# Chunk steps and layer head of a two-layer attention and RWKV-7 trunk: four moves of work in the engines' queues

## What is computed

```
x <- LN(alpha*x + (sigmoid(gA)*attention(x) + sigmoid(gB)*rwkv7(x)) @ w_out)
x <- LN(alpha*x + conv_glu(x))

attention:  8 heads of 128 share one k and v; an indexer scores the keys,
            the 64 best scores of each row are kept, softmax over these
rwkv7:      16 heads of 64; for each token t
   state = state*w_t + (state @ -kk_t) b_t + v_t k_t ;  y_t = state @ r_t
   kk_t  = k*k_k / |k*k_k|  (norm over a head)
   w_t   = exp(-exp(-softplus(-(w0 + tanh(p_w) @ w2)) - 0.5))
```

## Time and profile before

| | before |
|---|---|
| median of 3 runs | 1269.19 us (1268.2 to 1271.25) |
| the profiled execution's own time | 1277.04 us |
| its span | 1274.8 us |
| PE busy | 1160.5 us (91%) |
| DVE busy | 785.9 us (62%) |
| ACT busy | 537.2 us (42%) |
| granted TensorE clock, mean | 0.964 of full speed |
| HBM traffic over the span | 128 GB/s |

### The profile page before, as it was taken

One profiled execution on the slowest core, in us unless ns is written; L12 is line 12 of the kernel. 1 busy time (PEld: TensorE's weight loads), 2 busy tenths in 40 slices (PEclk: granted clock), 3 DMA queues, 4 the chain that ended last, 5 costly groups with the idle time before them and its releaser, 6 DMA issues.

```text
span 1274.8 us, 29251 instructions
## 1 busy us (share of the span) xinstructions
PE 1160.5 (91%) x12328; PEld 1042.2 (82%) x12328; DVE 785.9 (62%) x1436; ACT 537.2 (42%) x938; POOL 50.6 (4%) x56
## 2 busy tenths in 40 slices
PE   7996989898988899999999969898989898999997
PEld 7775878787878799998797758787878887999985
DVE  1338557675747777775522565667667577777745
ACT  2232445453534455654212424344545434556531
POOL 0000000000000100000000000000000001000000
PEclk9988999999999899999999978999999998999999
DMA  7422222222336365556464212212222464555561
GB/s 268 147 74 79 68 76 69 76 68 75 102 116 207 118 220 182 183 188 205 144 201 149 81 44 68 77 66 76 68 68 102 144 209 149 194 182 182 187 208 68
DMA packets 45353, 165.38 MB, mean 130 GB/s; under 512 B 5136, under 2 KB 5392, under 8 KB 44976
## 3 DMA queue, kind: packets, MB, share of 16 engines
q1 hardware_dynamic: 42576, 154.02, 36.3%
q0 software_dynamic: 1504, 7.47, 1.8%
q10 hardware_dynamic: 1152, 2.10, 0.5%
HBM read 160.42 MB, written 3.15 MB: 128 GB/s over the span
## 4 chain that ended last, share of the span: by engine, by line
PE 76%; DVE 17%; ACT 3%; issue 3%; DMA 1%; POOL 0%; DVEq 0%; SPq 0%; ACTq 0%
PE ps L722 18%; PE ps L723 16%; PE ps L724 16%; PE ps L869 8%; PE ps L697 5%; PE ps L1028 3%; DVE ring_r L1516 3%; DVE keep L1934 1%; PE ps L1070 1%; PE ps L881 1%; DVE small L1932 1%; PE ps L798 1%; PE ps L770 1%; ACT mid_hi L1192 1%; DMA ring<-stream_dram 1%
## 5 line engine op out<-in xcount | busy, mean ns | idle before, releaser
L722 PE MATMUL ps<-x_tok_r,mid_hi 128*128 128x256 f32 x448 | 138.6, 309 | 15.0 <-DVE ring_r L1516 15.0
L723 PE MATMUL ps<-xT_r,mid_hi 128*128 128x256 f32 x448 | 127.6, 285 | 0.0
L724 PE MATMUL ps<-x_tok_r,ring_r 128*128 128x256 f32 x448 | 127.4, 284 | 0.0
L722 PEld LDWEIGHTS ps<-x_tok_r,mid_hi 128*128 128x128 f32 x448 | 86.2, 192 | 25.3 <-issue 12.6
L697 PE MATMUL ps<-xT,ring 128*128 128x256 f32 x448 | 102.8, 388 | 0.0
L697 PEld LDWEIGHTS ps<-xT,ring 128*128 128x128 f32 x448 | 86.3, 195 | 13.8 <-issue 1.6
L1516 DVE TENSOR_TENSOR ring_r<-ring,mid_hi 128x1024 fp32r<-128x1024 f32 x64 | 77.9, 1219 | 25.0 <-ACT mid_hi L1192 25.0
L723 PEld LDWEIGHTS ps<-xT_r,mid_hi 128*128 128x128 f32 x448 | 86.7, 193 | 0.0
L724 PEld LDWEIGHTS ps<-x_tok_r,ring_r 128*128 128x128 f32 x448 | 86.5, 193 | 0.0
L1633 DVE COPY_PREDICATED X_Y<-masks,ps 128x256 f32<-128x256 uint32 x80 | 35.3, 441 | 66.0 <-PE ps L869 54.7
L1192 ACT CAST mid_hi<-ring 128x1024 fp32r<-128x1024 f32 x64 | 67.2, 1054 | 12.7 <-PE ps L724 12.7
(11 more groups left out here) (443 smaller groups left out, 3394.8 us busy)
## 6 DMA issues: line engine op xcount, KB each, us to landing
ring<-stream_dram SPq DMA_DIRECT2D x281, 512.0 KB, 3.4
lora_w<-lora_dram POOLq DMA_DIRECT2D x2, 1536.0 KB, 7.2
W_bt<-rpar_dram POOLq DMA_DIRECT2D x4, 512.0 KB, 4.5
kt_V<-rpar_dram POOLq DMA_DIRECT2D x4, 512.0 KB, 5.4
x_tok<-x_dram SPq DMA_DIRECT2D x2, 512.0 KB, 4.6
v_saved_dram<-vs_dC ACTq DMA_DIRECT2D x4, 256.0 KB, 3.9
x_tok<-x_dram SPq DMA_DIRECT2D x1, 1024.0 KB, 5.3
vf<-v_saved_dram ACTq DMA_DIRECT2D x4, 256.0 KB, 3.6
```

The costliest lines, as they stand in the source:

```text
L722: pe.matmul(dst, lh, rh, start=start, stop=False)
L723: pe.matmul(dst, lh, rl, start=False, stop=False)
L724: return pe.matmul(dst, ll, rh, start=False, stop=stop)
```

## The change

Seven edits, all of them moves; no instruction is added or taken out.

1. Head of a layer, PE: `prep_1` comes first, then two dense pieces, then `prep_ss` and `prep_v`; `prep_rnx` comes one place on, ahead of pieces 6 and 7. On DVE `prep_decay` and `prep_pend` come ahead of `prep_ss`.
2. `prep_bk` comes ahead of `prep_v` on DVE, in the head and in the last chunk step.
3. Softmax: `att_norm` comes ahead of level 3 on DVE (it stood after it).
4. `prep_ss` of the next group moves on PE from gap 13 to gap 12 (`SQUARES`).
5. Chunk steps: the splits due in a step come ahead of the Q copy on ACT, and ahead of the S sums on DVE, right behind Zs and T; T itself comes right behind Zs.
6. `prep_rnx` of the next group moves on PE from behind Z(1) and its fill to behind y(0), ahead of Z(1).
7. ACT resets Y at a group's start before it waits for v.

The lists of semaphore steps follow the new order and are left out. On PE:

```diff
-LOGITS, Y_BACK, BONUS, PROBS, VALUES = 4, 7, 8, 11, 13
+LOGITS, Y_BACK, BONUS, PROBS, SQUARES, VALUES = 4, 7, 8, 11, 12, 13
...
                     fill(14 + 2 * c)
-                    if g + 1 < GROUPS and c == 1:
-                        prep_rnx(r + 1)
...
                     mm.then_inc(*pe_wkv.inc(r, f"y{c}"))
+                    if g + 1 < GROUPS and c == 0:
+                        prep_rnx(r + 1)
...
-                for k, p in enumerate((prep_ss, prep_1, prep_v, prep_rnT)):
-                    p(r0)
+                for k, ps_ in enumerate(([prep_1], [prep_ss, prep_v], [prep_rnT], [prep_rnx])):
+                    for p in ps_:
+                        p(r0)
                     for piece in first[2 * k:2 * k + 2]:
                         piece()
-                prep_rnx(r0)
...
-                        gaps[VALUES].append(lambda: prep_ss(r0 + g + 1))
+                        gaps[SQUARES].append(lambda: prep_ss(r0 + g + 1))
```

On ACT:

```diff
             def chunk(r, c):
+                mids_up_to(r // GROUPS, mids_by(GAPS * (r % GROUPS) + 13 + 2 * c))
                 act.wait_ge(*pe_wkv(r, f"Q{c}"))
                 act.copy(Qs[:, :, :], step64(3)).then_inc(*act_wkv.inc(r, f"Q{c}"))
...
+                    act.copy(Y, stack.unsqueeze(1).broadcast_to([P, NU, CH])).then_inc(*act_wkv.inc(r, "resetY"))
                     act.wait_ge(*(dve_prep(r, "v") if l else dve_dense(l, ("rkv", 3 * g + 2))))
-                    act.copy(Y, stack.unsqueeze(1).broadcast_to([P, NU, CH])).then_inc(*act_wkv.inc(r, "resetY"))
...
                         chunk(r, c)
-                        mids_up_to(l, mids_by(GAPS * g + 14 + 2 * c))
```

On DVE (`chunk_t` makes T; `chunk_s` no longer does):

```diff
-                prep_ss(r0)
                 prep_decay(r0)
                 prep_pend(r0)
+                prep_ss(r0)
                 topk(0)
                 prep_rn(r0)
                 topk(1)
                 prep_keys(r0)
                 prep_arc(r0)
+                prep_bk(r0)
                 prep_v(r0)
-                prep_bk(r0)
...
                     for lev in range(LEVELS):
+                        if lev == 3:
+                            att_norm(l, g)
                         if lev:
                             level(r, lev)
...
-                        if lev == 3:
-                            att_norm(l, g)
...
                         if c:
                             chunk_z(r, c)
+                            if c < NCH - 1:
+                                chunk_t(r, c)
+                            mids_up_to(l, mids_by(GAPS * g + 13 + 2 * c))
...
                             elif nxt:
+                                prep_bk(r + 1)
                                 prep_v(r + 1)
-                                prep_bk(r + 1)
+                        else:
+                            mids_up_to(l, mids_by(GAPS * g + 13))
                         if c < NCH - 1:
                             chunk_s(r, c)
...
-                        mids_up_to(l, mids_by(GAPS * g + 13 + 2 * c))
```

More of the change, by code:

```diff
@@ L504, in trunk @@
         pool_att = by_layer("pool_att", ["eps", "rs"])
-        pe_prep = Steps(sem("pe_prep"), [["ss", "zw", "za"] + (["zv"] if r >= GROUPS else []) + ["rnT", "rnx"]
+        pe_prep = Steps(sem("pe_prep"), [(["ss", "zw", "za"] if r % GROUPS else ["zw", "za", "ss"]) + (["zv"] if r >= GROUPS else []) + ["rnT", "rnx"]
                                          for r in range(R)])
@@ L509, in trunk @@
                                            + (["thv"] if r >= GROUPS else []) for r in range(R)])
-        dve_prep = Steps(sem("dve_prep"), [["ss", "s", "cum", "cp", "pend", "rnT", "kkn", "k2", "kb", "arc"]
-                                           + (["v1", "v2", "v"] if r >= GROUPS else [])
-                                           + ["bneg", "kp", "rkk"] for r in range(R)])
+        dve_prep = Steps(sem("dve_prep"), [(["ss"] if r % GROUPS else []) + ["s", "cum", "cp", "pend"]
+                                           + ([] if r % GROUPS else ["ss"]) + ["rnT", "kkn", "k2", "kb", "arc", "bneg", "kp"]
+                                           + (["v1", "v2", "v"] if r >= GROUPS else []) + ["rkk"] for r in range(R)])
         pool_prep = by_round("pool_prep", ["rn"])
@@ L1673, in chunk_z, with chunk_t @@
                 dve.tensor_tensor(Zs[:, :, :], step64(2), akV[:, c::NCH, :], ALU.add).then_inc(*dve_wkv.inc(r, f"Z{c}"))
+            def chunk_t(r, c):
+                dve.tensor_tensor(Sa[:, :, :], S[:, (c + 1) % 2, :, :], ktV[:, GB * c:GB * c + GB, :], ALU.add
+                                  ).then_inc(*dve_wkv.inc(r, f"T{c}"))
             def chunk_s(r, c):
@@ L1677, in chunk_s @@
                 if c:
-                    dve.tensor_tensor(Sa[:, :, :], S[:, (c + 1) % 2, :, :], own, ALU.add).then_inc(*dve_wkv.inc(r, f"T{c}"))
                     dve.wait_ge(*dve_wkv(r, f"T{c}"))
```

## The result

The changed kernel took 1234.3 us (median of 4 runs, 1231.38 to 1236.45), the kernel before 1270.22 (4 runs, 1268.2 to 1271.99) beside it: a ratio of **0.9716**, interval 0.969 to 0.9742, faster. In a later study the pair stood at 1233.04 and 1273.85, ratio 0.9676 (0.9651 to 0.9702). So the gain is 35.9 us by the one pair and 40.8 by the other; the forecast's sum was 39.2.

The account below looks back on a forecast made before the run. PE's work plus its idle places was taken to bound the kernel. Heads 10.4 and 8.4, softmax 5.4, chunk steps 8.8 and clock 6.2 sum to 39.2 us, so 1269.2 us becomes 1230 us, range 1218 to 1246.

Parts of the forecast that it names:

- Bounds: Whole kernel: time is PE's work plus its idle places; PE busy 91% of the span, with 76% of the chain.
- Head of layer 0: From PE's idle at 78.88 us to DVE's first merge: search 8.7 us earlier, grams' start-up 1.7 less, 10.4 us gained.
- Head of layer 1: Same reordering from 711.48 us: search 5.4 us earlier, `b_k` ahead of v 2.1 more, first merge 8.4 us earlier.
- 717.5: Sign for layer 1's head: in the profile after, the search for the best starts near 717.5 us.
- Softmax: Division ahead of level 3: 1.0 us gained in four groups, 0.7 in two, 5.4 us, between 0 and 9.3.
- Chunk steps: Split waits 11.5 us gained, less 1.8 for Z(1) behind `prep_rnx` and 0.9 for `y_sum`: 8.8 us, between 0 and 11.5.
- The clock: Low stretches behind softmax waits, group 2 of layer 0 (4.2 us) and two layer 1 groups (1.0 each), go: 6.2 us.
- the last low clock before 439 us lies in group 0: Sign in the profile after: among layer 0's groups, the last low clock before 439 us is in group 0.
- the clock does not come back: Rival: low stretches arise elsewhere as often as they vanish; 10.8 us of gain lost, 1241 us; chance 0.15.
- DVE did not become the bound: Rival that DVE, fuller in chunk steps 1 and 2, becomes the bound: 8.8 and 5.4 us go, 1244 us; chance 0.13.
- ACT's rounding never held up Q: Slower rival: rounding ahead of the Q copy waits for its slot, up to 2.27 us per step, 1285 us; chance 0.03.
- nothing waited for a slot's landing: Rival that the stream's slots land too late, removed waits return as DMA waits, time stays near 1269; chance 0.02.

Follow-up runs that it names:

- head_only: The kernel before with only the heads' new order, bneg and kp ahead of v there, and ACT's earlier Y reset: 1250.01 us, ratio 0.9812.
- u_chunk: The change with the chunk steps' splits put back behind the Q copy on ACT and behind S on DVE: 1245.71 us, ratio 0.9799.
- rn_first: The change with DVE's copy of rnT moved ahead of the S(0) sums: 1223.36 us, ratio 0.9625.
- u_rnx: The change with `prep_rnx` put back behind Z(1) and its fill: 1227.14 us, ratio 0.965.
- b_fill: The kernel before with idle PE products added in the wait for the softmax's division, groups 1 to 3: 1267.47 us, ratio 0.9965.
- fill_head: The change with idle PE products added in the heads' wait for `b_k`: 1233.18 us, ratio 0.9678.

## Why the prediction was right, and where it was not

1230 us was forecast, 1234.3 measured, inside the range and faster as expected. The sum was helped by errors that cancelled, as told below. By steps:

- *Bounds.* Right: the time went with PE's waits and its clock. Of the profiles' last stage (324.96 to 319.76) some 2.5 us lie at no place that the change touches: head_only, which has every wait of that stage's group as before, took 322.51. They belong to the executions.
- *Head of layer 0*, 10.4 us. The search was forecast for 84.9 and began at 84.21; the operand's wait came out at 2.0 instead of 1.4 us, and the first merge was 11.1 us earlier. *Head of layer 1*, 8.4: 5.8 us for the search (5.4 forecast), 9.0 for the merge. The sign "717.5" was put in the old kernel's time; what was gained ahead of it had to come off, and the search began at 693.62. Together 19.8 of 18.8.
- *Softmax*, 5.4: 5.5 by the waits. What was named as late next, X_Y, is what is there, 0.75 us in four groups and 0.38 in two.
- *Chunk steps*, 8.8. Taken apart it was less good. The splits: 11.5 forecast, and 16.4 - 6.7 in `ring_r` plus 2.7 - 1.2 in the waits without a releaser give 11.2; taken back, 11.4. The longer wait for `y_sum` in layer 1: 0.9 forecast; the entry grew by 0.3. The wait behind `prep_rnx`: "0.3 us are lost in each of six groups, 1.8 us" is right as a wait (0.26 each), but edit 6 as a whole measured 7.2 (3.3 by the other ratio), of which 1.6 are the wait and 1.5 a low stretch. This term was too small, since the low clock behind the new wait was not in it.
- *The clock*, 6.2. **This is the step that failed**: "With the waits at 0.8 us or less I let these go." The low time in heads and groups fell from 64.9 to 30.7 us, but low stretches of 3.4 us stand behind waits of 0.75 us for X_Y in groups 1 and 2 of layer 0, and behind the new 0.82 us wait at L811 in group 1 of layer 1. So group 1 of layer 0 gained 1.1 us where the forecast's terms for it come to 1.0 + 1.5 - 0.3 = 2.2, and group 2 gained 5.4 of 6.4. Three such stretches at about 1.5 us are 4.5 of the 6.2. Group 0, where I had let the low clock stand, went the other way: from the grams' operand on it had 20.5 us at 0.50 in each layer and has 10.2, and its stages gave 3.1 and 2.6 us where the forecast's terms for them come to 1.2 and 0.9. The sign "the last low clock before 439 us lies in group 0" was wrong: it lies in group 2.
- *The sum.* The errors are of both signs, so the sum stands, at 39.2 against 35.9 and 40.8. That is in part luck: what the clock did not give back in groups 1 and 2 it gave in group 0, for which the forecast had nothing. Taken back one at a time the parts give 19.2 + 7.8 + 11.4 - 7.2 = 31.2; what is missing to 35.9 is less than four intervals of about 3 us leave uncertain, and with the change at a ratio of 0.969 in that study the parts would make up the whole.

Of the rivals, "the clock does not come back" was half right: low stretches did arise at other places, behind shorter waits, and 1234.3 lies between the forecast and its 1241. DVE did not become the bound in the steps (S's waits are as short as they were, but for the 0.26 us at L811), ACT's rounding never held up Q, and nothing waited for a slot's landing. The section of the Trainium skill that the prediction cited (TensorE: Matmul & The Clock Gate, HAM oscillation — how this bites in real kernels) gives as its rule that only idle gaps longer than any wait in these groups bring the low clock. The runs speak against that: a 1.8 us wait had 0.58 behind it, filled it had 1.00, and two of the 0.75 us waits have 0.82 behind them. In u_chunk the same 0.75 us wait in group 1 of layer 0 has no low stretch behind it, so the wait's length alone does not decide. The same section of the Trainium skill takes half of a throttled time as the price, by which I estimate 1.7 us for 3.4. The trace is near: the change's two profiles have 60.92 and 62.38 for one stage without such a stretch and with one, and rn_first and u_rnx have 59.29 and 60.72, 59.49 and 61.05 for the like stages of groups 2 and 1, so 1.4 to 1.6 us; for the 10.2 us behind the earlier trace rows it is 4.3 by b_fill, where half would be 5.1.

What stays open: how much edit 6 costs, 3 to 8 us; why the heads alone gave 23.8 where their rows give 19.8; what decides whether a wait of 0.75 to 1.8 us has a low stretch behind it; and edits 2 (in the chunk steps) and 7, which no run took back by themselves.

## What to carry to other kernels

On engines that run a queue in order, ask of each long wait what stands in the releasing engine's queue ahead of the releaser and is wanted later. Moving bulk work (a division, a split, v's three passes) behind a short operation that another engine waits for, or into time in which the engine is idle, gave nearly the waits' full sum here, and each of these terms could be read from the trace beforehand; that of the clock could not. When a step is moved on the waiting engine, move its partner on the releasing engine too: edit 6 lacked that, and one copy placed ahead of the sums took the loss away. And a wait with a low clock behind it is worth more than its length: in group 0, 2.3 us of wait were worth 4.

## What the runs showed of the hardware

- The granted clock fell to 0.50 for 3.4 us soon behind waits of 0.75 and 0.82 us. I had expected that of the 1.8 us waits and not of these.
- Two profiles of one kernel, with the same waits in the groups, had 30.7 and 37.5 us at the lower clock; the stage with the stretch more was 1.5 us longer.
- Products on unused data in a wait can shorten the kernel: b_fill does more work and takes 4.0 us less. In a place where DVE is the bound (fill_head) they gave nothing that could be measured, and the low clock came 1.9 us earlier.
- The same kernel against the same kernel before gave 0.9716 and 0.9676 in two studies, and profiled executions differ by up to 8 us from their median. A sum made against one profile carries that with it.
